# Deferred attention steps interleaved with an expert gather: another order of its scores, exponentials and weight copies, and a second copy of the values stored by head

## The reference, cut to what matters

```python
h  = rms_norm(x)
q, k, v, z, xbc, dt, gates = split(h @ w_in)
o_a = W_ao(diff_attention(q, k, v))        # 8 heads, two key maps each, ALiBi, mask by chunks of 64
o_s = W_so(ssm_branch(z, xbc, dt))         # convolution, SSD scan, gate, norm
x  += (sigmoid(g_a) * o_a + sigmoid(g_s) * o_s) @ w_out
x  += peer_ffn(rms_norm(x))                # 8 heads x 16 experts of 16384 for each row
x  += sigmoid(rms_norm(x) @ W_pg) * (p @ W_pe)
y   = rms_norm(x)

def diff_scores_apply(q, k, v, q_pos, k_pos, lam):
    s = einsum('bqhjd,bkhjd->bhjqk', q, k) * (A_DK ** -0.5)
    bias = -slopes[:, None, None, None] * abs(q_pos[:, None] - k_pos[None, :])
    a = softmax(where(mask, s + bias, NEG_INF), axis=-1)
    w = a[:, :, 0] - lam * a[:, :, 1]
    return einsum('bhqk,bkhd->bqhd', w, v)

def peer_ffn(h, ...):                      # for each row: top 16 experts of each of 8 heads
    pre = einsum('td,thkd->thk', h, u[idx])
    act = gelu(pre) * softmax(best scores)
    return einsum('thk,thkd->td', act, v[idx])
```

## Time and profile before

| | us |
|---|---|
| median of three executions | 4651.4 |
| the profiled execution, its own time | 4657.84 |
| its span in the trace | 4656.2 |
| early attention, from the trace | 1203 to 1402 |
| first fetch of an expert row | 1577.7 |
| deferred steps, from the trace | about 2092 to 2640 |

### The profile page before, as it was taken

The page is one execution under the profiler, slowest core; times in us unless marked ns, Lnnn a source line. Parts: engine busy times, 40 slices in busy tenths (PEclk is TensorE's granted clock), DMA queues, the critical chain, the costliest instruction groups (busy, mean ns, idle before and its releaser), DMA issues.

```text
span 4656.2 us, 52818 instructions
## 1 busy us (share of the span) xinstructions
PE 3684.8 (79%) x16970; PEld 2169.6 (47%) x16970; DVE 2820.1 (61%) x6369; ACT 1732.6 (37%) x5028; POOL 1489.1 (32%) x1390
## 2 busy tenths in 40 slices
PE   8999998999788887766777678887557766667668
PEld 7998777999657643423333223343122212222112
DVE  4443214777462486665777666667557766666774
ACT  2222112355460132335565432223334444444443
POOL 1000002333110143343343433344334444444442
PEclk9999999999899999988888889998778878888889
DMA  3223323665346699998999999999989999999996
GB/s 113 74 83 120 106 76 117 193 189 170 118 137 206 228 378 416 402 419 337 377 368 359 372 399 372 391 401 421 420 361 406 421 420 416 407 420 404 421 414 253
DMA packets 327109, 1409.05 MB, mean 303 GB/s; under 512 B 39216, under 2 KB 123200, under 8 KB 191680
## 3 DMA queue, kind: packets, MB, share of 16 engines
q0 software_dynamic: 167728, 1166.48, 62.1%
q1 hardware_dynamic: 159120, 239.35, 15.2%
HBM read 1324.55 MB, written 81.16 MB: 302 GB/s over the span
## 4 chain that ended last, share of the span: by engine, by line
PE 27%; DMA 23%; DVE 9%; ACT 4%; issue 4%; POOL 3%; another core or an unknown queue 0%; ACTq 0%; SPq 0%; DVEq 0%; POOLq 0%
DMA peer_uv<-in_peer_uv_dram,peer_idx 22%; PE peer_acc L3072 11%; PE peer_fo L2976 4%; DVE peer_uv L2203 3%; PE peer_fo L2989 3%; POOL peer_uv L2054 3%; PE peer_fo L2876 3%; PE peer_tb L2820 1%; ACT peer_space L2675 1%; PE peer_fo L3020 1%; PE peer_fo L3002 1%; ACT peer_scaled L2579 1%; ACT L2675 1%; PE peer_fo L2894 1%; DMA peer_space<-scratch_yg 1%
## 5 line engine op out<-in xcount | busy, mean ns | idle before, releaser
L2054 POOL DMA_INDIRECT peer_uv<-in_peer_uv_dram,peer_idx x1056 | 1222.5, 1158 | 1815.8 <-PE peer_acc L3072 1539.4
L3072 PE MATMUL peer_acc<-peer_uv,peer_scaled 128*64 128x512 f32 (+1 forms) x4224 | 1264.8, 717 | 625.0 <-ACT peer_scaled L2579 601.0
L2203 DVE CUSTOM_DVE_ANT_0 peer_uv<-peer_uv,peer_rep 128x1024 f32<-128x1024 f32 x1056 | 1279.0, 1224 | 783.1 <-DMA peer_uv<-in_peer_uv_dram,peer_idx 758.8
L3072 PEld LDWEIGHTS peer_acc<-peer_uv,peer_scaled 128*64 128x64 f32 (+1 forms) x4224 | 305.9, 156 | 1410.9 <-ACT peer_scaled L2579 836.4
L2574 ACT ACTIVATE peer_ge<-peer_pre 128x1 f32<-128x1 f32 x1056 | 212.5, 201 | 1586.2 <-DVE peer_pre L2203 1584.5
L100 PE MATMUL proj_bank<-proj_hTh,proj_wplead 128*128 128x352 f32 x1232 | 432.0, 351 | 1.8 <-DVE proj_wprest L92 1.8
L2976 PE MATMUL peer_fo<-peer_space 128*128 128x256 f32 (+2 forms) x1152 | 393.0, 489 | 49.2 <-DVE peer_space L2257 23.0
L2579 ACT ACTIVATE peer_scaled<-peer_eased,peer_ge 128x64 f32<-128x64 f32 (+1 forms) x1056 | 366.5, 347 | 122.5 <-ACT peer_ge L2574 3.2
L101 PE MATMUL proj_bank<-proj_hTr,proj_wplead 128*128 128x352 f32 x1232 | 401.7, 326 | 0.0
L102 PE MATMUL proj_bank<-proj_hTh,proj_wprest 128*128 128x352 f32 x1232 | 401.4, 326 | 0.0
L2572 ACT ACTIVATE peer_eased<-peer_fold,peer_gw 128x64 f32<-128x64 f32 (+1 forms) x1056 | 351.2, 333 | 25.9 <-DVE peer_gw L2185 25.9
(11 more groups left out here) (385 smaller groups left out, 5071.7 us busy)
## 6 DMA issues: line engine op xcount, KB each, us to landing
proj_wp<-in_w_in_dram POOLq DMA_DIRECT2D x13, 2048.0 KB, 10.0
peer_space<-in_w_ssm_o_dram SPq DMA_DIRECT2D x48, 512.0 KB, 7.0
proj_scan<-scratch_acum SPq DMA_DIRECT2D x36, 512.0 KB, 4.7
peer_uv<-in_peer_uv_dram,peer_idx POOLq DMA_INDIRECT x1056, 12.4
proj_wp<-in_w_in_dram POOLq DMA_DIRECT2D x14, 1024.0 KB, 9.0
peer_space<-in_w_attn_o_dram SPq DMA_DIRECT2D x24, 512.0 KB, 7.9
peer_space<-in_w_out_dram SPq DMA_DIRECT2D x24, 512.0 KB, 7.8
scratch_xtok<-proj_shared SPq DMA_DIRECT2D x20, 512.0 KB, 3.2
```

Source lines behind the costliest of these rows:

```text
L2054: pool.indirect_dma_start(uv[k][:], None, io["peer_uv"], bass.IndirectOffsetOnAxis(ap=idx[t % 2][:, col:col + 1], axis=0)).then_inc(uv_in[ ...
L2203: dve.tensor_tensor_reduce(uv[k][:, 0:D], uv[k][:, 0:D], rep[j][:], 1.0, 0.0, ALU.mult, ALU.add, pre[:, k:k + 1]).then_inc(u_done, 1)
L3072: x = pe.matmul(acc[group(t, slot % groups_of(t)), h:h + HALF], scaled[slot][:, 0:r], uv[slot][:, D + h:D + h + HALF], start=(it == 0 and ...
```

## The change

There are two parts.

**Order of the deferred steps.** The first score of a step moves from place 1 to place 0 and stands ahead of `values`, which moves from place 0 to place 1. The other three scores stay at 2 to 4, the turns at 5 and 6. DVE reads every score two places after its unit instead of one (places 2, 4, 5, 6), and combines at place 3. On ACT the copies of the turned halves and the scaled output are written out ahead of the exponentials in a place, and all move: the copies from 5 and 6 to 6 and 7 (7 is place 0 of the next step), the exponentials from 6 to 7, the output from 1 to 2. SP's loads of a head and stores of a step move by one place, the load after the last step by one slot, and the first unit after it by three.

**Values by head.** A new scratch tensor `vh` (1024 x 1024) holds for each head 128 rows of 4 KB, which are the partitions of `vt[b]`. `store` writes it with a fifth DMA in each head of the early attention, the count of `stored` goes from 64 to 80, and POOL waits for all five before it loads the next values into `vt[b]`. The deferred steps load values from `vh`.

```diff
 (early attention, gpsimd)
                         load_head(pool, b, i * (2 * P) + (2 + b) * P)
+                        hold(pool, gate, stored[b], (i + 2) * 80)
                         values_of(pool, b, i * (2 * P) + (2 + b) * P)
 (early attention, sync)
-                    sp.sem_inc(stored[b], 64)
+                    sp.sem_inc(stored[b], 80)
                     sp.dma_start(dr["att"][SEQ:T, cols], orow[b][0:DEC, NPT, :]).then_inc(stored[b], 16)
+                    sp.dma_start(dr["vh"][cols, :].rearrange("p (t d) -> p t d", d=P), vt[b][:, 0:NPT, :]).then_inc(stored[b], 16)
 (early attention, scalar)
-                    act.wait_ge(stored[b], (i + 1) * 64)
+                    act.wait_ge(stored[b], (i + 1) * 80)
 (retrieval, the table of units)
             for s in range(DSTEPS + 2):
+                if s < DSTEPS:
+                    units.append(("score", s, 0, 0, time, 1))
                 if s >= 2:
-                    units.append(("values", s - 2, 0, 0, time, 1))
+                    units.append(("values", s - 2, 0, 0, time + 1, 1))
                 if s < DSTEPS:
-                    units += [("score", s, n // 2, n % 2, time + 1 + n, 1) for n in range(4)]
+                    units += [("score", s, n // 2, n % 2, time + 1 + n, 1) for n in range(1, 4)]
                 if 1 <= s <= DSTEPS:
                     units += [("wturn", s - 1, n, 0, time + 5 + n, 1) for n in range(2)]
                 time += DSLOTS
-            D1 = time - DSLOTS + DTAIL
-            time += 1
+            D1 = time - DSLOTS + 1 + DTAIL
+            time += 4
     def exps_at(s):
-        return D0 + DSLOTS * s + 6
+        return D0 + DSLOTS * (s + 1)
     def combine_at(s):
-        return D0 + DSLOTS * s + 9
+        return D0 + DSLOTS * (s + 1) + 3
 (retrieval, sync)
-                    sp.dma_start(dv[b], io["v_prompt_out"].rearrange("(t p) c -> p t c", p=P)[:, :, cols]).then_inc(d_in[b], 16)
+                    sp.dma_start(dv[b], dr["vh"][cols, :].rearrange("p (t d) -> p t d", d=P)).then_inc(d_in[b], 16)
-                        if time == (D0 - 8 + h if h < 2 else D0 + DSLOTS * (ND * (h - 2) + ND + 1) + 1):
+                        if time == (D0 - 8 + h if h < 2 else D0 + DSLOTS * (ND * (h - 2) + ND + 1) + 2):
 (retrieval, vector)
-                        if kind == "score" and start - PE_AHEAD + 1 == time:
+                        if kind == "score" and start - PE_AHEAD + 2 == time:
 (retrieval, scalar)
                 def deferred(time):
+                    for n, (kind, s, half, _, start, _) in enumerate(units):
+                        if start - PE_AHEAD + 1 == time:
+                            if kind == "wturn":
+                                weights_turned_out(n, s, half)
+                            elif kind == "values":
+                                values_out(n, s)
                     for s in range(DSTEPS):
                         if time == exps_at(s):
                             exps_deferred(s)
-                    for n, (kind, s, half, _, start, _) in enumerate(units):
-                        if kind == "wturn" and start - PE_AHEAD == time:
-                            weights_turned_out(n, s, half)
-                        elif kind == "values" and start - PE_AHEAD + 1 == time:
-                            values_out(n, s)
```

5 lines of the change are left out of this document (3 added, 2 removed).

## The result

The changed kernel takes 4587.9 us (median of 4 runs, 4582.2 to 4593.6) against 4652.0 us before (median of 4 runs, the three of the prediction and one more, 4651.2 to 4653.1): a ratio of 0.9858, 95% interval 0.9847 to 0.9870. That is 64 us less. The nearest of the rivals is the first (4596), and it too is 8 us high. The profiled execution took 4593.6 us, its span is 4592.0.

The account below looks back on a forecast made before the run. The prediction found no engine full in the deferred window (DMA share 0.93), with waits between PE, ACT and DVE running the DMA engines dry. Terms 11 + 5 + 8 + 4 - 1 = 27 us took 4651.4 to 4624; range 4602 to 4652.

Parts of the forecast that it names:

- the first (4596): Rival, chance 0.12: breaking the loop of waits in the deferred steps fills the DMA engines and takes nearly all idle time; 4596.
- The ceiling: Deferred window: the same bytes at 410 GB/s take 488 us, not 548, so the order can give back 60 us.
- scores a place later: Deferred steps: DVE reads scores two places behind PE, halving its waits for them; 5 us gained, at most 13.
- Copies ahead of exponentials: ACT, deferred steps: copies of turned weights no longer wait for table load and exponentials; 11 us gained, bounds 0 and 17.8.
- 1.1 us of clock for each stall: Deferred steps: a less idle PE keeps more of the high clock, part of 2.2 us taken for each stall.
- the second rival: Chance 0.16: PE's waits for ACT's copies turn into waits for scaled weights, the first two terms give 0; 4642 to 4650.
- Values in 4 KB pieces: Deferred steps' loads of values: larger pieces save packet time and speed the gather beside them; 8 us gained, bounds 0 and 15.
- The fourth rival: Chance 0.18: the values' packets cost by bytes alone, so 4 KB pieces give nothing and the rest stands; 4632.
- Values land as fast as keys: Sign of being right: deferred values, landing in 22.1 us before, land as fast as same-sized keys, 7.0 us.
- After the last step: First unit behind the deferred steps: two slots further from its row loads, cutting PE's 17.33 us wait; 4 us gained.
- The fifth store, 1 us lost: Early attention: SP issues one more DMA of about 0.5 us a head, exposed once before the stage's final barrier.
- The third (PE before a full bank): Rival, chance 0.10: PE waits for DVE to empty score banks in the deferred steps; 38 us lost against 27 gained, 4662.

## Why the prediction was wrong, step by step

**The ceiling was right** and was nearly reached. 60 us was stated for the window, and the change got 55 there and 9 just behind it. Idle DMA time in 2092 to 2640 was 38.6 us before and is 1.9 now. The rest came from the rate per full share, 392 to 407 GB/s by the 4 us slices.

**The step that failed is the sizing of "scores a place later"**: 5 us were taken, with a bound of 13, and the edit alone gives 41. The working had first given the idle time to other causes (17.8 us to seven stalls behind ACT's copy, 7 us to the row load) and left 13 us for DVE. But the view of waits had shown DVE standing 110.4 us for scores, in 38 places, and the run with the later read alone, with the one that put the copies first, shows that the idle time belonged to DVE's stalls: it followed them and not PE's waits for copies (38.6, 55.9 and 9.8 us in the second table above). In the stall of the earlier trace rows DVE stood 6.84 us before a score; the prediction read it as the end of a chain that begins at ACT. It was the link that counted. DVE takes the dots of all slots in order, and gelu, scaled weights, PE pair and fetch of a slot follow from them; while it stands before a score, no further slot's dots are taken. With the read one place later PE may be as late as before, behind the same copies (47.7 us of waits), and DVE goes on with dots. That the later read removes most of the loss is shown; the path through the dots is read from the order of the work and the waits, not measured by itself.

**"Copies ahead of exponentials", 11 us, is worth nothing.** Alone it costs 23 us, together with ACT's later place it gives nothing that can be told (-3), and taken back from the changed kernel it changes nothing. PE's wait for the copies, the largest of PE's waits, could be cut or put back without a gain or a loss of that kind; that the eight slots in flight cover it is a reading, not measured. The 1.1 us of clock for each stall that this term held do not show either: the granted clock of the window is 0.88 before and after. The check on offer was the second rival's sentence, that the wait would only change its name: it did (85.2 us for scaled weights). Its forecast of 4642 to 4650 (the low end should be 4640, for 4651 - 11) failed since it left "scores a place later" at nothing as well.

**"Values in 4 KB pieces", 8 us:** the size holds for the part alone (8), by luck, and is 15 on top of the new order; the reason was wrong in the main. The rate of the gather depends on them by about 1% (392 against 395, 404 against 407 and 404 against 409 GB/s per full share), which over 488 us is an estimated 5 us, where the prediction had reckoned up to 15. What they cost before was mostly SP's queue: issues of 5.36, 2.46, 2.35 and 5.28 us, and 16.18 us of PE behind a load of rows that had to follow. The fourth rival, that the pieces give nothing, was nearly right on the rate and wrong on the time. "Values land as fast as keys" failed too: 13.9 against 8.1 us in the run with the weighing moved, better than 22.1 but not equal:

```profile
peer_space<-scratch_chan SPq DMA_DIRECT2D x6, 512.0 KB, 8.1
peer_space<-scratch_vh SPq DMA_DIRECT2D x6, 512.0 KB, 13.9
```

Whether the values gain more beside the new order (15 us, about 5 to 24) than alone (8 us, 2 to 14) isn't settled, for the intervals overlap. The run with the order alone still holds the row wait (15.39 us of PE), which may cost more in a pipeline without other slack, and the 1% of the rate counts for more when the engines are full; no run takes the row wait alone out of the new order.

**"After the last step", 4 us,** with bounds 0 and 5: 8 us by the run that takes it back, -1 to 18 by the intervals; the fetches of the changed kernel gain 9 us there. The wait came to 6.19 us where 12 had been foreseen.

**The fifth store, 1 us lost, and the new wait at nothing** were right: 0.6 us, with PE's use of the values 0.12 us later.

**Order parts that were costed at nothing.** The first score ahead of the values was not priced at all. Alone it costs 7 us, ACT's later place alone gives 3, and the two together 25: each makes the other engine's place fit. The parts fail to add in the other direction too: the pair (-25), the later read (-41) and the later turn (-8) would make -74, and the order as a whole gives -51, at a DMA share of 0.99 where little is left to gain. The prediction treated each edit as a term of a sum, and the reordering isn't one.

**The rivals.** The first (the DMA engines fill up) is what happened; it had a chance of 0.12 because DVE's blocks and the row load seemed untouched. The row load was touched, through SP's queue. DVE's blocks of top-k work are still there at a share of 1.00; that they fit into the eight slots once DVE's reads of scores no longer stand in line with them is a reading, not tested alone. The third (PE before a full bank) is real, but not at this distance: PE's scores and turns wait 16 us for DVE in the changed kernel and 72 with one place more. Its price, 0.29 us of time for each us of wait, was too low: 30 us were lost on 55 more of such waits, 0.5 for each, with ACT's waits behind them included.

**What is open.** Why the changed kernel with scores one place behind is at -50, when its parts give -25 (pair), -8 (turn) and -8 to -15 (values), is covered by these sums within their intervals, but not closely. Whether ACT's later place is worth 10 us in the changed kernel or nothing, one run with a wide interval does not tell.

## What to carry to other kernels

Among waits, ask first which engine takes the first step of every slot, in order (here DVE with its dots), and price the places where that engine stands before side work; the longest wait of an engine further down can be free. Test it by removing each wait alone, since a sum of terms did not hold here. A distance of one more place between producer and reader is cheap to try and has an optimum: here one, two and three places gave -50, -66 and -36 us. And a DMA rate per full share below the later one isn't proof that small pieces cost bandwidth: raise the share by another means and see how far the rate follows (here from 392 to 404 GB/s, and the last 1% was the pieces').

## What the runs showed of the hardware

Loads in 1024 pieces of 512 bytes slowed the traffic beside them by about 1% (404 against 409 GB/s per full share at the same DMA share of 0.98), and held the issuing queue: the four issues behind the first of two such loads took 2.35 to 5.36 us in place of 0.4, and the values themselves landed in 22.1 us before, and in 29.7 us with scores two behind, against 7.0 and 7.7 us for keys of the same size. The Trainium skill, "DMA: Bandwidth & Descriptors", section "Queues, rings and completion order", says that each DMA engine takes turns between the queues, a packet at a time; that a small piece waits for its turn beside the gather's would agree with the landing times, but no run here varies the number of pieces alone on an idle queue.
